# A hybrid decoder step on one core: a third expert fixed by number, three blocks of 96 slots in front, and one exchange near the end of the block order

## The reference

```python
eid = grp[:, None] * EXP_PER_GROUP + top_i          # two experts for each token, 2064 rows in all
def run_block(args):
    e, toks, w = args                               # up to 128 token rows of expert e
    xb = x_pad[toks]
    h = jax.nn.silu(xb @ w_gate[e]) * (xb @ w_up[e])    # 1024 -> 512
    return (h @ w_down[e]) * w[:, None].astype(xb.dtype)  # 512 -> 1024
y = jnp.zeros((t + 1, D_MODEL), xt.dtype).at[slot_tok].add(yb.reshape(n_slots, D_MODEL))[:t]
```

## Time and profile before

| | |
|---|---|
| Median of 3 runs | 1719.39 us (1716.16 to 1719.78) |
| Profiled execution | 1711.8 us, span 1710.0 us |
| TensorE matmul busy | 1642.7 us, 96% of the span |
| VectorE, ScalarE, GpSimd busy | 661.3, 339.4, 163.9 us |
| DMA | 337.67 MB, mean 197 GB/s over the span |
| Granted TensorE clock, mean | 0.98 |

### The profile page before, as it was taken

The page is one execution under the profiler, slowest core; times in us unless marked ns, Lnnn a source line. Parts: engine busy times, 40 slices in busy tenths (PEclk is TensorE's granted clock), DMA queues, the critical chain, the costliest instruction groups (busy, mean ns, idle before and its releaser), DMA issues.

```text
span 1710.0 us, 22521 instructions
## 1 busy us (share of the span) xinstructions
PE 1642.7 (96%) x9285; PEld 1009.8 (59%) x9286; DVE 661.3 (39%) x1395; ACT 339.4 (20%) x670; POOL 163.9 (10%) x169
## 2 busy tenths in 40 slices
PE   7999999999999999999999999999999999999990
PEld 5556777777777666666688555654444444444440
DVE  1446464544542323232477745551111212121225
ACT  1113222323231221222122000101111111111115
POOL 1000000000002422111000000001111111111110
PEclk9999999999999999999999999989999999999995
DMA  7201121121027445443263443289999999999975
GB/s 229 62 18 24 50 63 50 52 61 50 13 75 210 170 148 172 140 136 112 65 235 125 187 160 136 101 302 390 391 392 377 392 395 391 381 389 396 389 268 203
DMA packets 104410, 337.67 MB, mean 197 GB/s; under 512 B 24378, under 2 KB 68482, under 8 KB 87924
## 3 DMA queue, kind: packets, MB, share of 16 engines
q1 hardware_dynamic: 89572, 276.22, 43.0%
q0 software_dynamic: 13568, 55.78, 10.8%
q10 hardware_dynamic: 1168, 4.23, 0.6%
HBM read 307.90 MB, written 35.51 MB: 201 GB/s over the span
## 4 chain that ended last, share of the span: by engine, by line
PE 91%; DMA 5%; DVE 2%; issue 1%; ACT 1%; POOL 0%; SPq 0%; DVEq 0%; POOLq 0%; ACTq 0%
PE psum L1075 12%; PE psum L1189 10%; PE psum L1515 8%; PE psum L1520 7%; PE psum L1377 6%; PE psum L1392 5%; PE psum L1541 4%; PE psum L1116 4%; PE psum L1547 4%; PE psum L979 3%; PE psum L1228 3%; PE psum L1089 2%; DMA arena<-in_w_up 2%; PE psum L1134 2%; PE psum L1528 2%; PE psum L1123 2%
## 5 line engine op out<-in xcount | busy, mean ns | idle before, releaser
L1075 PE MATMUL psum<-arena 128*128 128x258 f32 x896 | 215.3, 384 | 0.0
L1189 PE MATMUL psum<-arena 128*128 128x344 f32 x576 | 182.3, 458 | 0.0
L1075 PEld LDWEIGHTS psum<-arena 128*128 128x128 f32 x896 | 162.9, 190 | 27.9 <-issue 7.0
L1520 PE MATMUL psum<-arena 128*64 128x512 f32 x320 | 141.6, 595 | 0.0
L1521 PE MATMUL psum<-arena 128*64 128x512 f32 x320 | 141.6, 595 | 0.0
L1515 PE MATMUL psum<-arena 128*128 128x512 f32 x320 | 139.8, 595 | 1.1 <-DVE arena L2552 1.1
L1189 PEld LDWEIGHTS psum<-arena 128*128 128x128 f32 x576 | 103.3, 190 | 52.9 <-issue 11.2
L1515 PEld LDWEIGHTS psum<-arena 128*128 128x128 f32 x320 | 60.0, 190 | 73.6 <-issue 73.2
L1377 PE MATMUL psum<-arena 128*128 128x258 f32 x448 | 99.9, 387 | 0.9 <-ACT arena L1802 0.9
L1392 PE MATMUL psum<-arena 128*128 128x512 f32 x224 | 99.2, 596 | 0.0
L1377 PEld LDWEIGHTS psum<-arena 128*128 128x128 f32 x448 | 86.6, 194 | 14.3 <-issue 1.3
(11 more groups left out here) (394 smaller groups left out, 2125.6 us busy)
## 6 DMA issues: line engine op xcount, KB each, us to landing
arena<-in_w_gate SPq DMA_DIRECT2D x32, 2048.0 KB, 24.7
arena<-in_w_up SPq DMA_DIRECT2D x32, 2048.0 KB, 30.3
arena<-in_w_down SPq DMA_DIRECT2D x32, 2048.0 KB, 30.6
arena<-in_w_in SPq DMA_DIRECT2D x33, 512.0 KB, 5.3
gates<-arena SPq DMA_DIRECT2D x16, 516.0 KB, 6.1
arena<-gates SPq DMA_DIRECT2D x16, 516.0 KB, 6.6
arena<-in_x_prompt SPq DMA_DIRECT2D x16, 512.0 KB, 4.5
arena<-in_w_o SPq DMA_DIRECT2D x1, 4096.0 KB, 17.6
```

The costliest lines, as they stand in the source:

```text
L1075: ins = mm(psum[:, BANK[name[0]], 0:QT], held, moved, start=(k == 0 and name in ("X1", "V6", "Y5")), stop=(k == 3), skip_group_check=True)
L1189: ins = mm(psum[:, FB + t, 0:SP3], wring[:, u, k, :], xT[:, k, t * SP3:(t + 1) * SP3], start=(k == 0), stop=(k == KD - 1))
L1520: g = mm(psum[0:64, 2, :], xgT[:, xpar, k, 0:64], wg[:, k, :], start=(k == 0), stop=(k == KD - 1))
```

## The change

The first three blocks work on experts 0, 1 and 2, with 96 slots each (before: experts 0 and 1, with 128 slots each, and a third block of 64 slots for a ranked expert). The ranks move with it: 8 blocks of 128 slots (before 10), 13 of 96 (10), 9 of 64 (10), 2 of 32 (2). In the written order the kinds of the blocks 3 to 26 are what they were; the last two blocks of 128 and 96 slots of the string, "hmfmqq", become "hfmmqq", so that block 27 is an F and block 28 a T. In SyncE's queue the three loads of block 2 are issued for expert 2, without a read of the order, ahead of the wait for ord_dve; the third of them (load 8) still waits for block 0's gate. `width`, which turns a rank into a number of slots on VectorE and is called twice, has one step more.

```diff
-        FIXED, FULL, MID, LOW = 2, 10, 20, 30
+        FIXED, FULL, MID, LOW = 3, 11, 21, 30
-        RANK = list(range(FIXED)) + [next(kinds[c]) for c in "hhfmhfmhfmhmhfmhfmhfmhfmhmfmqq"]
+        RANK = list(range(FIXED)) + [next(kinds[c]) for c in "hfmhfmhfmhmhfmhfmhfmhfmhfmmqq"]
...
         def full(n):
-            return RANK[n] < FULL
+            return FIXED <= RANK[n] < FULL
 
         def three(n):
-            return FULL <= RANK[n] < MID
+            return RANK[n] < FIXED or FULL <= RANK[n] < MID
...
-            sp.wait_ge(ord_dve, 1)
+            for m in range(2):
+                load_matrix(3 * SOON + m, SOON)
 
             def expert_at(n):
                 return sp.value_load(order[0:1, RANK[n]:RANK[n] + 1].bitcast(I32), min_val=0, max_val=NE - 1)
 
-            for n in range(SOON, NE):
+            load_matrix(3 * SOON + 2, SOON)
+            sp.wait_ge(ord_dve, 1)
+            for n in range(FIXED, NE):
                 e = expert_at(n)
                 for m in range(3):
                     load_matrix(3 * n + m, e)
...
             def width(out, by):
 
                 link(ts(out, by, float(FULL), None, ALU.is_lt))
+                link(stt(out=out, in0=by, scalar=float(FIXED), in1=out, op0=ALU.is_ge, op1=ALU.mult))
                 link(stt(out=out, in0=by, scalar=float(MID), in1=out, op0=ALU.is_lt, op1=ALU.add))
                 link(stt(out=out, in0=by, scalar=float(LOW), in1=out, op0=ALU.is_lt, op1=ALU.add))
```

## The result

| | before | after |
|---|---|---|
| Median | 1717.90 us (5 runs, 1715.53 to 1719.78) | 1727.57 us (5 runs, 1725.69 to 1729.61) |
| Profiled execution | 1711.8 us, span 1710.0 | 1728.11 us, span 1726.0 |
| TensorE matmul busy | 1642.7 us | 1653.6 us |
| Granted TensorE clock, mean | 0.98 | 0.97 |

The ratio is 1.0056 (95% interval 1.0041 to 1.0071): 9.7 us slower. The forecast was 1719.9 us, in a range from 1715.1 to 1725.0. A second set of 6 runs, beside new runs of the kernel before, gave 1.0079 (1.0059 to 1.0100). The two profiled executions differ by more than the medians, 16.0 us of span: the one of before was quick, 6.1 us under its median. So what a part costs is taken from medians and ratios, and where the time goes from the profiles.

What follows compares the result with a forecast made beforehand. TensorE was taken to set the pace until the weight stream's lead is gone near the end. Block 28's down +0.9, scalings +1.0 and add -1.4 gave +0.5 us on the 1719.4 us median: 1719.9 us, range 1715.1 to 1725.0.

Steps and rivals of the forecast that it cites:

- the term for the weight stream: Front loads: DMA engines idle 8 us between loads 7 and 8; load 10 lands +1.5 us, bounds -0.6 to +3.
- the early loads: SyncE's queue in front: loads 6 and 7 leave 9.5 us earlier, near 1106.2 us; the time won is lost before load 8.
- the fall of the clock: Tables and next turn: 3.4 us at half clock after the idle time cost 1.7 us; bounds nothing and 5.1 us.
- The prediction's own sign of being wrong: Wrong if tables start without a gap, TensorE waits for weights several times in the body, or load 10 lands over 3 us off.
- The first step: Whole kernel: TensorE and DMA engines both full; TensorE sets the pace until the first late weight wait, near the end.
- Rival 3: Whole kernel: weight stream alone sets the end; sum +0.1 us, 1719.5 us; chance 0.60 together with the main sum.
- Block work: First three blocks: 96 slots each instead of 128, 128, 64 save 4.4 us of TensorE work.
- The gap: Before the slot tables: TensorE idles 4.5 us waiting for VectorE's one-hot steps; tables begin at 1137.7 instead of 1136.5 us.
- The tail: Blocks 27, 28 and last adds: block 27's wait goes; down +0.9, scalings +1.0, add -1.4, together +0.5 us.

Runs made afterwards that it cites:

- loads 8 and 9 late: The kernel before, with loads 8 and 9 issued only once the slot lists stand; 1725.59 us, 1.0061.
- tables first: The changed kernel with loads 6 and 7 behind the wait for the expert order and VectorE's one-hot table steps ahead of block 0's gate product; 1.0025, again 1.0018.
- late loads: The changed kernel with loads 6 and 7 again issued behind the wait for the order of experts; 1723.73 us, 1.0046.
- filled gap: The changed kernel with loads 6 and 7 behind the order wait, plus 4.1 us of unused matmuls before the slot tables; 1721.91 us, 1.0038.
- early loads alone: The kernel before with expert 2 fixed and loads 6 and 7 issued early; blocks of 128, 128, 64 slots and old end order; 1721.20 us, 1.0039.
- swap alone: The kernel before with only the end order changed: block 27 gets 128 slots, block 28 gets 96; 1.0009.
- fixing alone: The kernel before with expert 2 fixed by number and one more VectorE step in width; sizes, load times and end order unchanged; 1.0013.
- first block of 128: The changed kernel with loads 6 and 7 behind the order wait and blocks of 128, 96, 96 slots in front; 1719.65 us, 1.0024.

## Why the prediction was wrong, point by point

The step that failed is the term for the weight stream: load 10 was put at +1.5 us, with -0.6 to +3 as bounds, and was 12.4 us late. Under it lie two others: the early loads, priced at nothing, which held up the first gather (10.04 us for 3.3), and the fall of the clock, put at 1.7 us and measured at 5.9. The prediction's own sign of being wrong, load 10 over 3 us off, came true.

**What bounds the kernel.** The first step read the few waits of TensorE as "TensorE sets the pace", and rated the stream as full but not ahead. Both are full in the body, but it is the stream that sets the end: with TensorE's work from block 0 to block 4 untouched (loads 8 and 9 late), 13.5 us more of idle DMA time ended the kernel some 11 us later by the profile (615.3 against 604.3 us from load 5) and 10.5 us by the medians. The 20% of empty front was named ("a start (1105 to 1144 us) in which the DMA engines are not full") and then not priced as a loss that can grow. Rival 3 had this mechanism, but took load 10 at +1.5 us, so it came to 1719.5.

**Block work.** Right in size: a T's rest at full clock, down and halves measured as their rows. The 4.4 us were not won: tables first, which keeps them and has no gap, is 1.0025 and 1.0018, and its TensorE, 4.7 us sooner at block 4 in one profile, waits 4.7 us longer for weights.

**The gap.** Right: 4.5 us. But it began from a later point. Tables start 1144.89 - 1126.99 = 17.9 us after block 0, where 10.6 + 2.0 + 3.4 = 16.0 was worked out; 1.75 us of the difference is the rest of block 0 at half clock (5.35 us for 3.6). With late loads, where that rest took 3.66 us, it is 1141.20 - 1125.00 = 16.2 us.

**The clock.** Mis-sized. 1.7 us taken, 5.1 the bound; measured 8.72 - 4.68 = 4.0 us in the tables and 5.42 - 3.59 = 1.8 us in the rest of block 1, 5.9 us together, over a stretch of 12.1 us at 0.50. TensorE came to block 4 8.4 us later, counted from block 0 (78.8 us for 70.35), where 2.4 us were forecast. The term took the shortest stretch of the trace, "since the work that follows is dense"; the dense work didn't end it for 12.1 us. A second such fall stands behind the wait at block 28, where the 64 small matmuls took 5.34 us for 3.59. The rule that was weighed, the Trainium skill, "TensorE: Matmul & The Clock Gate", section "HAM oscillation" (a data wait between bursts of matmuls makes the next burst start cold), holds at both gaps, though the first was a wait for VectorE and not for data, and the filled gap, at 1.00, shows it from the other side.

**The early loads.** Their times were right, 0.6 and 1.0 us behind load 5. What failed is that they were priced only on their own queue. The first gather of GpSimd goes 7.6 us after load 5, and now three loads (6 MB) have been issued ahead of it instead of one: 10.04 us instead of 3.3, a wait of 1.5 us here and of 3.8 in the early loads alone. In the swap alone the gather goes 7.6 us after load 5 too, with load 5 alone ahead of it, and takes 3.2 us. The step asked what the two loads precede in SyncE's queue and not what they meet from GpSimd's. Cost of the part: 1.0039 against 1.0013 for the fixing alone, 4.5 us; with tables first 1.0054 against 1.0025, 5.0 us. The Trainium skill, "DMA: Bandwidth & Descriptors", section "Queues, rings and completion order", says that each DMA engine takes turns between the queues that have work, a packet at a time. The trace agrees in part: the gather landed at 1124.95, 1.7 us ahead of load 7 (issued 1108.24, 18.5 us), so it did not wait for the whole queue; it took three times as long all the same, and no run here shows how the turns were shared.

**The weight stream.** The term that was most off. Idle time between loads 7 and 8 was forecast at 8 us and measured at 11.5. It was set down as "the time won in front is lost", that is as nothing, because load 10 was taken to depend on the slot lists alone (+1.5, bounds -0.6 to +3). Load 10 was issued 12.4 us late: 5.3 from the later start of block 0, 3.05 from there to the tables, 4.04 in the tables. It landed at 1162.9 us, +11.1. The start of block 0 is in part no effect of the change: profiles with the front of before have it between 1121.69 and 1126.87, and the gather itself was issued 7.6 us after load 5 here and 5.5 us after it before. Counted from load 5, load 10 is 10.8 us late.

**The tail.** The wait at block 27 went, as forecast. Block 28 waited 3.9 us, forecast at most 2 and none in the sum. Its add took 11.09 us for 13.09, -2.0 for -1.4. All of it was right in kind and made no difference, since the same exchange in the kernel before gives 1.0009.

**The account of the 0.56 to 0.79%.** Early loads 0.26% (early alone less fixed alone). Gap and clock 0.21 to 0.28% (late loads less tables first, both runs). Each of these differences has an interval of about 0.2 points to either side, so that the parts are known to about their own size only. What is left in tables first, 0.18 to 0.25%, is the fixing (0.13%, may be zero) and the sizes in front, of which the profiles show the later release of the gate places: 2.2 us of idle DMA time behind block 0 with tables first, 1.8 us in block 2 with a first block of 128. The parts add up to 0.65 to 0.79%. That they add up so well is in part luck. How the last part divides stays open: its intervals all overlap. Whether TensorE's lateness by itself, with a full DMA queue, costs anything was not tried.

## What to carry to other kernels

Where two engines are both full in the body, find the stage in front where one of them is idle while the other is busy, and price it: here each us of idle DMA time went with about a us of the end, and the waits of the busy engine didn't show it. Before moving a transfer earlier, list the transfers of other queues that are issued in the next 10 us and have a waiting engine behind them. A smaller block that releases its buffers all at once, at its end, can leave the stream of loads idle for longer than a larger one that releases the first half way (2.2 us here); what this alone cost in time was not separated.

## What the hardware showed that was not expected

The clock's level in the thin work ahead of block 0 differs from one execution of the same kernel to the next. The kernel before recovered to 1.00 from 1103.8 to 1110.5 us in one profile and from 1107.5 to 1114.0 in the other; with the same front and loads 8 and 9 late it stayed at 0.50 from 1101 to 1124 us, and block 0 came at 1126.87 instead of 1121.69 or 1123.38. The time follows the mean granted clock of an execution: over all timed runs, within each kernel, 0.001 less of it goes with 1.25 us more (for the kernel before, 1709.6 to 1710.2 us at 0.982 and 1720.1 to 1721.5 at 0.974). Half clock for 3.4 us is 0.001 of the mean and costs TensorE 1.7 us, so this is near what the matmuls lose (an estimate). Of the 0.7% spread of the kernel before, most is this, and a single profile of a kernel can therefore be 5 us off in its front alone. Counting from the issue of load 5, the two profiles of the kernel before agree within 0.1 us. This doesn't always help: the two of tables first are 7.4 us apart even so (603.6 and 611.0 us), since the clock was still at another level behind load 5, and block 0 began 3.6 us later in the second.
